# Fourteen more projection slices as seven products of halves, in a one-core layer of linear recurrences and mixture of experts

## The reference

```
proj = x @ w_in          # 1024 -> lru_x, lru_y (1024 each), ml_q, ml_k (256), ml_v, ml_o (512), gd_q,k,v,z (512), gates (3072)
xa = causal_conv(lru_x) + b;  ha = rg_lru(xa) * gelu(lru_y);                br_a = ha @ w_br_lru
hb = rms_norm(mlstm(ml_q, ml_k, ml_v)) * sigmoid(ml_o);                      br_b = hb @ w_br_ml
q,k,v = silu(causal_conv(gd_q|gd_k|gd_v)), q and k normalised
hc = rms_norm(gated_delta(q, k, v)) * silu(gd_z);                            br_c = hc @ w_br_gd
x = layer_norm(a * x + (g0 * br_a + g1 * br_b + g2 * br_c) @ w_out)
x = layer_norm(a * x + moe(x))
```

## Time and profile before

| | us |
|---|---|
| median of 3 runs (lowest to highest) | 1292.63 (1292.39 to 1293.22) |
| profiled execution | 1292.72 |
| its span | 1290.9 |
| TensorE busy | 1247.0 |
| VectorE, ScalarE, GpSimd busy | 375.3, 163.7, 103.3 |
| read from HBM | 460.68 MB |

### The profile page before, as it was taken

The page is one execution under the profiler, slowest core; times in us unless marked ns, Lnnn a source line. Parts: engine busy times, 40 slices in busy tenths (PEclk is TensorE's granted clock), DMA queues, the critical chain, the costliest instruction groups (busy, mean ns, idle before and its releaser), DMA issues.

```text
span 1290.9 us, 18843 instructions
## 1 busy us (share of the span) xinstructions
PE 1247.0 (97%) x8098; PEld 684.6 (53%) x8098; DVE 375.3 (29%) x821; ACT 163.7 (13%) x283; POOL 103.3 (8%) x89
## 2 busy tenths in 40 slices
PE   9999999999999999999999999999899999999896
PEld 8888889999864344344343443434243333434342
DVE  4857583553443120211202112121111112120213
ACT  1441621121030000000000000000000000000001
POOL 1000035644100000000000000000000000000001
PEclk9999999999999999999999999999999999999999
DMA  7645227357899999999999999999999999999995
GB/s 271 204 136 181 102 99 293 123 216 289 327 368 423 421 429 409 427 426 427 427 414 428 427 428 425 428 427 427 426 428 429 425 430 428 428 426 429 428 428 238
DMA packets 51180, 463.06 MB, mean 359 GB/s; under 512 B 11896, under 2 KB 13840, under 8 KB 17072
## 3 DMA queue, kind: packets, MB, share of 16 engines
q1 hardware_dynamic: 45280, 459.85, 86.6%
q10 hardware_dynamic: 5840, 2.32, 0.7%
HBM read 460.68 MB, written 1.47 MB: 358 GB/s over the span
## 4 chain that ended last, share of the span: by engine, by line
PE 68%; DMA 20%; issue 1%; POOL 0%; DVE 0%; ACT 0%; POOLq 0%; SPq 0%; DVEq 0%
PE ps L1164 26%; DMA mix<-expert_w 10%; PE ps L1182 10%; DMA ring<-expert_w 10%; PE ps L684 7%; PE ps L1061 4%; PE ps L1073 4%; PE ps L707 4%; PE ps L1157 3%; PE ps L984 2%; PE ps L718 1%; PE ps L1173 1%; PE ps L808 1%; PE ps L1191 1%; PE ps L937 0%
## 5 line engine op out<-in xcount | busy, mean ns | idle before, releaser
L1164 PE MATMUL ps<-ring,mix 128*64 128x512 f32 x1512 | 338.3, 592 | 0.1
L1164 PEld LDWEIGHTS ps<-ring,mix 128*64 128x64 f32 x1512 | 106.5, 137 | 194.8 <-issue 190.6
L1182 PE MATMUL ps<-ring,mix 128*64 128x512 f32 x752 | 170.1, 594 | 19.5 <-DMA ring<-expert_w 19.5
L707 PE MATMUL ps<-mix 128*128 128x256 f32 x736 | 162.1, 380 | 0.0
L707 PEld LDWEIGHTS ps<-mix 128*128 128x128 f32 x736 | 138.7, 190 | 19.7 <-issue 1.2
L2176 DVE TENSOR_SCALAR mix<-ps 128x512 f32<-128x512 f32 x32 | 22.1, 692 | 370.6 <-PE ps L1164 370.6
L1164 PE MATMUL ps<-mix 128*64 128x512 f32 x536 | 121.1, 593 | 3.9 <-DMA mix<-expert_w 3.7
L1182 PEld LDWEIGHTS ps<-ring,mix 128*64 128x64 f32 x752 | 53.0, 137 | 120.5 <-issue 98.0
L2185 DVE COPY mix<-ps 128x512 f32<-128x512 f32 x32 | 22.1, 692 | 240.6 <-PE ps L1173 240.6
L647 POOL TENSOR_TENSOR mix<-mix 128x1024 f32<-128x1024 f32 (+1 forms) x2 | 3.4, 1700 | 955.9 <-ACT mix L1592 955.9
L1164 PEld LDWEIGHTS ps<-mix 128*64 128x64 f32 x536 | 37.6, 137 | 77.0 <-issue 69.8
(11 more groups left out here) (294 smaller groups left out, 940.1 us busy)
## 6 DMA issues: line engine op xcount, KB each, us to landing
ring<-expert_w SPq DMA_DIRECT2D x121, 2048.0 KB, 30.7
mix<-expert_w SPq DMA_DIRECT2D x39, 2048.0 KB, 29.7
mix<-stream_w SPq DMA_DIRECT2D x42, 1024.0 KB, 4.9
ring<-expert_w SPq DMA_DIRECT2D x41, 1024.0 KB, 10.0
mix<-expert_w SPq DMA_DIRECT2D x22, 1024.0 KB, 21.8
mix<-stream_w SPq DMA_DIRECT2D x8, 512.0 KB, 4.2
mix<-first_w SPq DMA_DIRECT2D x4, 512.0 KB, 4.9
mix<-planes ACTq DMA_DIRECT2D x1, 1024.0 KB, 7.2
```

The lines of the kernel that those rows point to most:

```text
L707: ins = mm(o[:, m * S:(m + 1) * S], w[:, c, m * P:(m + 1) * P], XT[c] if rhs is None else rhs[:, c, :], start=(m == 0 and c == 0), stop=(c ...
L1164: ins = mm(PS[64 * a:64 * a + 64, bank + g, :], XE[j][:, c, 64 * a:64 * a + 64], w[a][:, g * 512:g * 512 + 512], start=False, stop=(c == K ...
L1182: ins = mm(PS[64 * a:64 * a + 64, bank + h, :], HT[:, c // 4, c % 4, 64 * a:64 * a + 64], w[a][:, h * 512:h * 512 + 512], start=(c == 0), ...
```

## The change

`lx0-3`, `ly0-3`, `mq`, `mk`, `mo0-1` (called early) and `gz0-1` are multiplied in halves too. For the early ones ScalarE copies "a" to the destination and "b" to one of two buffers `PB3`, GpSimd joins the parts (`finish`, six operations) and counts `combined`; whoever reads the slice waits for that count. ScalarE's copy of a "b" waits until the join two slices earlier has released `PB3`. The sigmoids of `mo` are taken after the join. The `gz` slices are joined by VectorE with `whole`, as the gates are. GpSimd's order becomes: sums of a slice, join of the one two slices before it, and so on. The token sums of the LRU branch move from GpSimd to VectorE (`branch_sums`), the first LRU convolution moves behind the heads on VectorE, several buffers get other homes, and the early load of `TAIL` and the later load of place 5 change places, the first with a wait for the third update of the delta state.

```diff
 def halved(name):
-    return name[:2] == "ga" or name[:3] == "br0"
+    return name[:2] in ("ga", "gz") or name[:3] == "br0" or early(name)
+def early(name):
+    return name[:2] in ("lx", "ly", "mq", "mk", "mo")
...
                 if name == "ga11":
                     full(sp, closing("br03"))
-                    sp.dma_start(TAIL, ...)
+                    sp.wait_ge(E("state"), NC)
+                    load_steps(5, 0, 5)
...
             full(sp, closing("ga23"))
-            load_steps(5, 0, 5)
+            sp.dma_start(TAIL, ...)
...
+            def finish(name, dst):
+                i = early_at[name]
+                moved(gp, name + "a")
+                moved(gp, name + "b")
+                corners, middle = dst
+                b = PB3[i % 2]
+                nc_g.tensor_tensor(PSUMS, middle[:, 0, :], middle[:, 1, :], ALU.add)
+                nc_g.tensor_tensor(corners[1], corners[0], corners[1], ALU.add).then_inc(E("pool_own"), 1)
+                gp.wait_ge(E("pool_own"), 3 * i + 1)
+                nc_g.tensor_tensor(middle, middle, corners[1].unsqueeze(1).to_broadcast([P, 2, P]), ALU.add
+                                   ).then_inc(E("pool_own"), 1)
+                gp.wait_ge(E("pool_own"), 3 * i + 2)
+                nc_g.tensor_tensor(corners[1], corners[1], PSUMS, ALU.add)
+                nc_g.tensor_tensor(corners[0], corners[0], b[:, 0, :], ALU.add)
+                nc_g.tensor_tensor(middle, middle, b[:, 1:3, :], ALU.add).then_inc(E("pool_own"), 1)
+                gp.wait_ge(E("pool_own"), 3 * i + 3)
+                gp.sem_inc(E("combined"), 1)
...
+            weight_sums(at("lx0"))
+            weight_sums(at("lx1"))
+            for n in range(4):
+                weight_sums(at(f"lx{n + 2}" if n < 2 else f"ly{n - 2}"))
+                finish(f"lx{n}", padded(n))
             gp.wait_ge(E("gsilu_v"), 1)
             clear(X_, 0.0)
             clear(XTi, 0.0)
+            for n in range(4):
+                weight_sums(at(f"ly{n + 2}" if n < 2 else ("mq", "mk")[n - 2]))
+                finish(f"ly{n}", flat(LY, n))
+            finish("mq", flat(QM, 0))
+            finish("mk", flat(MK, 0))
...
-            gp.wait_ge(E("ha_ready"), 1)
-            moving_sums(4, HAS, ...)
-            gp.wait_ge(E("mss"), 2 * NT)
-            for i in range(len(in_halves)):
+            weight_sums(at("mo0"))
+            weight_sums(at("mo1"))
+            for n in range(2):
+                weight_sums(at(f"gz{n}"))
+                finish(f"mo{n}", flat(MO, n))
+            for i in range(at("ga00"), len(in_halves)):
                 weight_sums(i)
...
+            def both_parts(name, dst, scale=1.0):
+                i = early_at[name]
+                full(act, name + "a")
+                nc_s.mul(dst, ps(name + "a")..., scale).then_inc(free(name + "a"), 1)
+                if i >= 2:
+                    act.wait_ge(E("combined"), i - 1)
+                full(act, name + "b")
+                nc_s.mul(PB3[i % 2]..., ps(name + "b")[:, 0:3 * P], scale).then_inc(free(name + "b"), 1)
...
-            evac("mo1", MO[:, 2:4, :], func=ACT.Sigmoid)
-            for n in range(2):
-                full(act, f"gz{n}")
-                A(GZ..., ps(f"gz{n}")..., ACT.Sigmoid).then_inc(E("zsig"), 1)
+            evac("mo1", MO[:, 2:4, :])
+            for n in range(2):
+                act.wait_ge(E("combined"), early_at[f"mo{n}"] + 1)
+                A(MO..., MO..., ACT.Sigmoid).then_inc(E("zsig"), 1)
+            for n in range(2):
+                first_part(f"gz{n}", GZ...)
+                moved(act, f"gz{n}b")
+                A(MT[n], GZ..., ACT.Sigmoid).then_inc(E("zsig"), 1)
...
             def conv_lru(n):
-                moved(dve, f"lx{n}")
+                dve.wait_ge(E("combined"), early_at[f"lx{n}"] + 1)
...
             def gelu_argument():
-                for n in range(4):
-                    moved(dve, f"ly{n}")
+                dve.wait_ge(E("combined"), early_at["ly3"] + 1)
...
             def mlstm_gate():
-                for n in range(2):
-                    moved(dve, f"mo{n}")
+                dve.wait_ge(E("zsig"), 2)
...
             mlstm_gate()
+            branch_sums()
             silu_z(0)
             silu_z(1)
```

More of the change, by code:

```diff
@@ L234, in layer_kernel @@
     in_halves = [name for name, _, _ in stream if halved(name)]
+    early_at = {name: n for n, name in enumerate(name for name in in_halves if early(name))}
+    late_at = {name: n for n, name in enumerate(name for name in in_halves if not early(name))}
     def stream_value(n):
@@ L336, in layer_kernel @@
         MSQ = area(MIX, 106.5, 1024).rearrange("p (t h n) -> p t h n", t=NT, h=MH)
-        HAS = [area(MIX, 112 + 2 * n, 512).rearrange("p (c n) -> p c n", n=P) for n in range(4)]
-        WS = [[area(base, kb, 512).rearrange("p (c n) -> p c n", n=P) for base, kb in homes]
-              for homes in (((MIX, 106.5), (MIX, 108.5), (RING, 88)), ((RING, 90), (RING, 92), (RING, 94)))]
+        HAS = [area(RING, 88 + 2 * n, 512).rearrange("p (c n) -> p c n", n=P) for n in range(4)]
+        WS = [[area(MIX, 111 + 6 * k + 2 * n, 512).rearrange("p (c n) -> p c n", n=P) for n in range(3)] for k in range(2)]
+        PB3 = [area(MIX, 123 + 1.5 * n, 384).rearrange("p (q n) -> p q n", n=P) for n in range(2)]
+        PSUMS = area(MIX, 126, P)
         MG = area(MIX, 56.25, 2048).rearrange("p (c s) -> p c s", s=S)
@@ L628, in _, with flat, padded @@
             moving_sums(0, [v.rearrange("p (a b) n -> p a b n", a=2) for v in XS], *xq)
+            def finish(name, dst):
[15 more added lines that the diff above has]
+                gp.sem_inc(E("combined"), 1)
+            def flat(tile, n):
+                q = tile[:, 2 * n:2 * n + 2, :].rearrange("p c s -> p (c s)").rearrange("p (q n) -> p q n", n=P)
+                return (q[:, 0, :], q[:, 3, :]), q[:, 1:3, :]
+            def padded(n):
+                rows = LX[:, 2 * n:2 * n + 2, :].rearrange("p b s -> p (b s)")
+                return ((rows[:, 3:3 + P], rows[:, 2 * 259 - P:]),
+                        rows[:, 3 + P:3 + P + 2 * (P + 3)].rearrange("p (q n) -> p q n", n=P + 3)[:, :, 0:P])
+            at = in_halves.index
+            weight_sums(at("lx0"))
[3 more added lines that the diff above has]
+                finish(f"lx{n}", padded(n))
             gp.wait_ge(E("gsilu_v"), 1)
@@ L763, in _ @@
                 proj(f"gq{n}")
+            pe.wait_ge(E("moving_sums"), 4)
             for n in range(2):
@@ L1450, in _ @@
             A(LU, LU, ACT.Sqrt).then_inc(E("lu"), 1)
-            evac("mo0", MO[:, 0:2, :], func=ACT.Sigmoid)
+            evac("mo0", MO[:, 0:2, :])
             for t in range(NT):
@@ L1472, in first_part @@
                 nc_s.copy(dst, ps(name + "a")).then_inc(E("part_copied"), 1)
+            for n in range(2):
+                first_part(f"gz{n}", GZ[:, 2 * n:2 * n + 2, :].rearrange("p c s -> p (c s)"))
+                moved(act, f"gz{n}b")
+                A(MT[n], GZ[:, 2 * n:2 * n + 2, :].rearrange("p c s -> p (c s)"), ACT.Sigmoid).then_inc(E("zsig"), 1)
+            gates = [f"{n}{d}" for kind, n, d in branch_items() if kind == "ga"]
             def gate(k):
@@ L1704, in _ @@
             dve.sem_inc(E("heads"), 1)
+            conv_lru(0)
             conv_lru(1)
@@ L1862, in mlstm_gate, with whole, branch_sums @@
                 dve.sem_inc(E("hb_ready"), 1)
-            def silu_z(n):
[L1865 to L1869, removed]
+            def whole(name, dst):
+                three = dst.rearrange("p (q n) -> p q n", q=4)
+                dve.wait_ge(E("part_copied"), late_at[name] + 1)
+                step(tt(three[:, 3, :], three[:, 0, :], three[:, 3, :], ALU.add))
+                step(tt(three[:, 1:3, :], three[:, 1:3, :], three[:, 3:4, :].to_broadcast([P, 2, P]), ALU.add))
+                tt(three[:, 3, :], three[:, 1, :], ps(name + "a")[:, 2 * P:3 * P], ALU.add
+                   ).then_inc(free(name + "a"), 1)
+                moved(dve, name + "a")
+                full(dve, name + "b")
+                tt(dst[:, 0:3 * P], dst[:, 0:3 * P], ps(name + "b")[:, 0:3 * P], ALU.add).then_inc(free(name + "b"), 1)
+                moved(dve, name + "b")
+            def silu_z(n):
+                z2 = GZ[:, 2 * n:2 * n + 2, :].rearrange("p c s -> p (c s)")
+                whole(f"gz{n}", z2)
+                dve.wait_ge(E("zsig"), 3 + n)
+                step(stt(z2, z2, VC[:, V_GG:V_GG + 1], MT[n], ALU.mult, ALU.mult))
+            def branch_sums():
+                b11, b12, b21, b22 = [LY[:, 4 * k:4 * k + 4, t * P:(t + 1) * P] for k in range(2) for t in range(NT)]
+                for n, (dst, left, right) in enumerate(((HAS[0], b12, b11), (HAS[1], b22, HAS[0]), (HAS[2], b22, b12),
+                                                        (HAS[3], b21, HAS[1]))):
+                    tt(dst, left, right, ALU.subtract).then_inc(E("moving_sums"), 1)
+                    dve.wait_ge(E("moving_sums"), 4 + n + 1)
```

24 lines of the change are left out of this document (10 added, 14 removed).

## The result

The changed kernel takes 1337.68 us, median of 4 runs (1337.34 to 1338.0), against 1292.93 (1292.39 to 1293.46) for the kernel before beside it: a ratio of 1.0346, 95% interval 1.0328 to 1.0364, or +44.7 us. The forecast was 1331 in 1304 to 1344. The profiled execution has a span of 1335.5 us.

What follows compares the result with a forecast made beforehand. TensorE sets the pace until the expert-load burst at 340.54 us, remaining DMA bytes after it. gz1's delay, net of savings, +36.5 and clock +1.8 make +38.3 us on 1292.7: 1331 us, range 1304 to 1344.

Steps and rivals of the forecast that it cites:

- Where the time is made: Whole kernel: a microsecond TensorE wins or loses before the expert-load burst at 340.54 us moves the end by a microsecond.
- TensorE's saving: Fourteen slices multiplied in halves: 0.66 us each, 9.2 us, most swallowed where TensorE waits.
- GpSimd's price: Per slice: weight sums 5.35 us and join 3.3 us, 8.65 us against TensorE's 6.25.
- rival B: Slower joins: 128-element additions 0.6 us, 256-element 0.9, each join 1.1 us longer; 1341 us; chance 0.10.
- VectorE held: Chained VectorE operations with two SBUF operands each take a GpSimd turn: 1.41 us beside a 512-element sum.
- The ladder: From the convolutions to mv0, delays pass between engines: lx2 +9.5, inverted blocks +28.1, mv0 +25.5 us.
- The wait at gz1: gz1 needs gz0's bank, freed behind the mLSTM gate and branch subtractions: starts 37.1 us later, TensorE idle 13.7 us.
- T: The end of mo1 on TensorE, forecast at 203.2 us; gz1 was to start 20.8 us after it.
- Clock: Half clock after the idle before gz1: 3.6 us of matmuls cost 1.8 us; earlier idles taken at 0.
- A: GpSimd's pace without the shared port, VectorE running free beside it: +14 us, 1307 us; chance 0.14.
- C: In the convolutions, VectorE's scalar_tensor_tensor isn't held by GpSimd: 1321 us; chance 0.10.
- D: GpSimd keeps ahead of every use, gz0's bank frees in time, all 9.2 us stay: 1283.5 us; chance 0.05.

Runs made afterwards that it cites:

- warm_short: Changed kernel with 40 idle 128x128 matmuls on TensorE in its wait for gz1's bank: 1338.29 us.
- gz_first: Changed kernel with gz0's first part copied ahead of mo's sigmoids and gz0 joined ahead of the mLSTM output gate: 1327.17 us.
- all_free: free_gz_first with the weight sums of lx0 and lx1 left out too, so GpSimd does nothing for the fourteen slices; output invalid: 1285.29 us.
- free_gz_first: free_helper with gz0's join moved ahead of the mLSTM output gate; output invalid: 1292.77 us.
- free_helper: Changed kernel without GpSimd's joins and its added weight sums except lx0 and lx1; expert rounds held at one, output invalid: 1303.12 us.
- g_adds: Kernel before with 68 unneeded 128x512 SBUF-to-SBUF additions on GpSimd: 1320.79 us.
- g_sets: Kernel before with GpSimd kept as busy as in g_adds, but by memsets that read no SBUF: 1293.7 us.
- late_best: Changed kernel with only mo and gz in halves, the order of gz_first, and gz1 behind the u and w products: 1296.84 us.

## Why the prediction was right

**Where the time is made.** Right: the burst moved by 44.4 us and the end by 44.7. One addition from warm_short: a gain before 240 us can still be lost at GpSimd's sums of the last gates, as its 2.9 us were. The 11.1 us that gz_first had won at ga00 reached the end as 10.5.

**TensorE's saving** was put at 9.2 us and at next to nothing in the end. all_free shows 8.1 of it where next to nothing stands in the way, and free_gz_first shows that eight sums eat nearly all of it.

**GpSimd's price.** Most sums have turns of 1.33 to 1.43 us; those of mo0 and mo1, which TensorE doesn't wait for, take 7.25 and 7.54 us for four. The additions of 128 elements, which no row had shown, mostly take 0.45 to 0.64 us (0.46 was taken). The ten joins up to 162 us span 3.3 to 5.2 us, 3.9 in the mean (3.3 taken, 4.4 in rival B), and three of them are over the 4 us that the prediction had named as a sign against itself. So B had half its lengthening.

**VectorE held.** Right, and this was the step that decided. The unknown, the scalar_tensor_tensor, is held like the addition. The shares foretold came too: GpSimd was busy for 81% of 38 to 145 us, TensorE for 78% of 60 to 230.

**The ladder**, predicted and measured: decay arguments 106.8 and 107.43, inversion 131.8 and 132.69, inverted blocks 143.9 and 147.01, lg 150.1 and 153.41, mv0 164.3 and 168.41, end of mo1 203.2 and 207.5. lx2 had 74.9 and 76.67; 0.6 of these 1.8 us is the opening's, and 1.1 was gone by the decay arguments. The mis-sized term is the inversion, +5 on 7 us where it took +7.2 (14.3 us): GpSimd, which I had running dry after ten turns, had half a join, four sums and a whole join left, until 143.7 us. And the clock behind the idle ahead of lg was taken at 0: lg and what follows took 15.0 us to mv0 where 14.2 were forecast, lg itself 10.17 us at a granted clock of 0.70, where its two halves had taken 7.34 (3.62 in the earlier trace rows and 3.72). By mv0 that makes 4.1 of the 6.4 us that the forecast lacked, by the end of mo1 4.3; the wait at gz1 adds 1.2 and the clock behind it 0.7.

**The wait at gz1.** Right in its mechanism and its length from T: 22.0 us for 20.8; the chain of waits of the changed kernel (start us, us, what) goes through the very steps of the sum:
```profile
207.68 1.51 POOL mix L633
...
212.49 2.13 POOL mix L633
...
218.18 0.64 ACT mix L1525
...
219.68 4.11 DVE mix L1915 x3
...
225.37 0.70 DVE ring L1948
```
GpSimd's sums of gz1 took 6.9 us there, not 5.35, for they are held by VectorE's scans as much as they hold them. TensorE's idle was 10.8 us and not 13.7, because mt had waited 3.1 us already, which the prediction had not seen. What it left unsaid is that about half of this idle time needs no GpSimd at all (of the 7.75 us in free_helper 2.4 are GpSimd's), and that the order alone mends nearly all of it.

**Clock.** 1.8 us were forecast, 2.5 measured (8.94 against 6.42 for gz1). The place was right; the lower level lasted longer than the 3.6 us of matmuls taken for it (the clock was 0.71 over 8.9 us). For the earlier idles the prediction named the same price and took it at 0, since another engine ends what follows them. That held in part: at lg 2.8 us of slower matmuls (10.17 against 7.34) moved mv0 by 1.2 against lg, and the waits at mt and gz1, 3.3 us in all, cost gz1 1.8 us in gz_first (8.22 against 6.42).

**Rivals.** A fell to g_adds against g_sets, B in its size to the joins' rows (half of it is there), C to the row at 86.36 us, D to the wait at gz1. D is the case that all_free builds by force, and it gives 1285.3 where 1283.5 had been worked out.

## What to carry to other kernels

Work given to an idle engine is not free if it holds up one on the chain: 12 us of GpSimd additions cost this kernel about 7 us, while memsets that filled far more of its time cost nothing. Price a helper by the number of its turns that meet chained VectorE operations, each lengthened to a whole turn, and not by its own busy time. When a product's bank is freed by an addition on another engine, put that addition ahead of all work that doesn't concern it: the order alone was worth 10 us here.

## What the runs showed of the hardware

- A chained VectorE operation with two SBUF inputs takes one turn of a GpSimd sum: 0.51 us become 1.42 beside the changed kernel's sums of 512 elements, and 1.19 in g_adds, whose turns are 1.17. tensor_tensor_scans are held too, 0.61 us to 1.1 (4.49 for four) and 1.6 (6.47 for four). Beside GpSimd's memsets (g_sets) scalar_tensor_tensors are free, and a tensor_scalar from SBUF to SBUF takes 0.80 for 0.35.
- The holding goes both ways: a GpSimd sum of four operations takes 5.3 us where VectorE is quiet and 6.93 beside its scans.
- The second product group of the opening, the same 32 matmuls in every kernel, took 7.07 to 8.42 us in the profiles (7.12 before, 7.72 in the changed kernel). In late_best its first eight records take 0.40 us each, about twice the 0.22 of the group's pace in the kernel before. The granted clock reads 1.00 there in both. What makes it so is open. A difference of 1 us between two single profiles need not be an effect of the code.
